# Moving the output gate of the last six expert rows to GpSimd, and the residual add to TensorE

## The chip, the cores and the metric

The program runs on one core of a Trainium2 chip. The metric is the device time of one execution in microseconds (us). TensorE is called PE, VectorE DVE, ScalarE ACT, GpSimd Pool, and the engine that only starts transfers here SP. PE's two clock levels are 1.2 and 2.4 GHz; a granted clock of 1.00 is the higher one.

## The reference, cut to what matters

Two transformer blocks over 256 tokens of width 1024. Only the very end of the second block is touched: a product-key mixture of single-neuron experts, its gated addition to the residual, and the last norm.

```python
def peer_ffn(h, ...):                      # 8 heads, 16 picks each, 16384 experts
    ...
    def chunk(args):                       # 128 tokens
        xc, ec, wc = args
        u = expert_u[ec]
        a = jax.nn.gelu(jnp.einsum('cd,chkd->chk', xc, u), approximate=False) * wc
        return jnp.einsum('chk,chkd->cd', a, expert_v[ec])
...
x = x + gt2[:, None, :] * peer_ffn(modulate(rmsnorm(x, norm2_g), sh2, sc2), ...)
return rmsnorm(x, final_g)
```

So each token needs 8 x 16 = 128 expert rows (u and v side by side, 2 x 1024 floats), a dot product of the u half with the token, a weight, and a weighted sum of the v halves; the sum is multiplied by the gate vector gt2, added to the residual, and the row is normed.

## The kernel before, in words

The first 870 us are two dense blocks and the attention of the second. Then comes the stage of the expert rows. The work is cut into 16 *units*: unit j is head j % 8 of token block j // 8 (128 tokens, one to a partition). A unit has 16 *picks*. For each pick Pool starts one indirect transfer (`fetch`, L2172) that brings for each of the 128 tokens its own row of 8 KB: 1 MB a pick, 256 picks in all. The rows land in 16 buffers (names in the rows: `arena`, `ring`, `rows_w`, `rows_x`, `rows_s`, `rows_l`); Pool may start a fetch when PE has read the pick that held the buffer before.

For each pick, in this order:

- DVE multiplies the u half with the token's vector and sums it (`dots`, L2014, a custom operation that reads two operands in SBUF).
- ACT takes the gelu of the sums of a group of picks (L1456), and DVE multiplies it with the softmax gate (`weigh`, L2025).
- ACT turns the weight of each token into a 128 x 128 diagonal matrix (`activate`, L1463; the diagonals lie in the buffers `silu` and `pT`).
- PE multiplies this diagonal with the v half in two halves of 512 columns (`weigh`, L1053 and L1057), and the sums grow in two PSUM banks: 4 and 5 for the first token block, 6 and 7 for the second. The fp32 product runs as two passes, so each half is two records.

Picks are taken in groups of 4, in the last unit in groups of 4, 2, 2, 2, 2, 1, 1, 1, 1 (`pick_groups`).

The order is written out by hand on each engine. PE's picks run in loops (`Fori`) of one unit a turn. Early in the stage `turn_residual` (L1046) transposes the residual h of both token blocks into banks 0 to 3. For the first token block, `total(0)` and `scaled_first` run between later units. For the second, after the last pick, `total(1)` on DVE takes for each half of 512 columns the sum from PSUM times the gate row (`gtrow`, in the tile `small`; L2036) and adds the turned residual from PSUM (L2037); ACT squares and sums the result (`finish`, L1472) and takes the root (L1477); DVE multiplies the row by the final gain (`fgrow`, L2059), inverts the root (L2047) and scales one half (L2063), ACT scales the other (L1528); SP and ACT each start one half's output transfer (L477, L1530).

Before this change Pool's last instruction is the start of the last fetch.

Of the kernel before, what the change touches and what calls it, by code (L numbers as in the profile page):

```python
# [14 lines left out]
P = 128  # L15
T = 256
TB = T // P
D = 1024
# [122 lines left out]
LOOPED = 2  # L141
assert all(HOMES[g][0] == HOMES[g - TK][0] for g in range((LOOPED + 1) * TK, UNITS * TK))

# [53 lines left out]
def program(nc, a, out):  # L197
    with ExitStack() as ctx:
# [181 lines left out]
        def _(sp):  # L380
# [96 lines left out]
            sp.dma_start(out[P:T, 0:512], out_rows[:, 1, 0:512]).then_inc(S("stored"), 16)  # L477
# [4 lines left out]
        def _(pe):  # L482
# [558 lines left out]
            def turn_residual():  # L1041

                pe.wait_ge(S("banks_freed"), S_END)
                for b in range(TB):
                    for c in range(C):
                        last = nc.tensor.transpose(ps[:, 2 * b + c // 4, (c % 4) * P:(c % 4 + 1) * P],  # L1046
                                                   h[:, c, b * P:(b + 1) * P], ident)
                last.then_inc(S("residual_turned"), 1)

            def weigh(acc, j, k, rows, first=False):  # L1050
# [4 lines left out]
                if k == TK - 1:  # L1055
# [33 lines left out]
            with pe.Fori(PH + 1, 2 * PH) as j:  # L1089
                weigh_unit(6, j)  # L1090


        @block.scalar
        def _(act):
# [370 lines left out]
            def finish(b):  # L1465
# [3 lines left out]
                for x in range(2):  # L1469
                    at = slice(x * 512, (x + 1) * 512)  # L1470
                    act.wait_ge(S("summed"), 2 * b + x + 1)
                    fn(squares[:, 2 * x:2 * x + 2, :], out_rows[:, b, at].rearrange("p (k n) -> p k n", k=2), ACT.Square,  # L1472
# [54 lines left out]
            act.wait_ge(S("gained"), 2)  # L1527
            fn(out_rows[:, 1, 512:D], e["junk"][:, 512:D], ACT.Copy, scale=lb[:, 7, 1:2]).then_inc(S("second_ready"), 1)  # L1528
            act.wait_ge(S("second_ready"), 1)
            act.dma_start(out[P:T, 512:D], out_rows[:, 1, 512:D]).then_inc(S("stored"), 16)  # L1530
# [3 lines left out]
        def _(dve):  # L1534
# [493 lines left out]
            def total(b):  # L2028

                for x in range(2):  # L2030
                    at = slice(x * 512, (x + 1) * 512)
                    if x == 0:
                        dve.wait_ge(S("half_weighed"), (b + 1) * PH)
                    else:
                        dve.wait_ge(S("weighed"), (b + 1) * PH * TK)
                    own(v.tensor_tensor(e["junk"][:, at], ps[:, 4 + 2 * b + x, :], gtrow[:, at], ALU.mult))  # L2036
                    own(v.tensor_tensor(out_rows[:, b, at], e["junk"][:, at], ps[:, 2 * b + x, :], ALU.add))  # L2037
                    dve.sem_inc(S("summed"), 1)

                dve.wait_ge(S("squares_summed"), 2 * b + 1)  # L2040
# [252 lines left out]
```

## Time and profile before

| | |
|---|---|
| median of three runs | 1518.01 us (1517.78 to 1518.86) |
| profiled execution, its own time | 1517.04 us |
| its span, first to last instruction | 1515.2 us |
| mean granted clock of PE | 0.975 |
| PE busy | 1372.2 us (91%) |
| DVE busy | 974.2 us (64%) |
| ACT busy | 554.8 us (37%) |
| Pool busy | 557.3 us (37%) |
| DMA, whole run | 427.03 MB, mean 282 GB/s |

The device time is 1.8 us longer than the span, which runs from the first to the last instruction seen. Busy shares are averages over stages with different limits; the change lies in the last 30 us, and what counts there is read from that stretch.

### The profile page before, as it was taken

To read this page: it belongs to the slowest core of one execution; us is meant where nothing else is said; L and a number is where in the kernel's file an instruction comes from. 1 tells how busy PE (TensorE), PEld (TensorE's weight loads), DVE (VectorE), ACT (ScalarE), POOL (GpSimd) and SP (SyncE) were. 2 spreads that over 40 slices of the span, in tenths; PEclk is the share of its full clock that TensorE was granted. 3 is DMA by queue.
4 is the path that set the end of the run, shared out by engine and by line. 5 is a ranking of instruction groups with operands and counts; after the bars stand their busy time and mean duration, and the time that the engine had idled before them with its cause. 6 is when DMAs were issued, how large, how long until landed. Compare 5 with 4: busy or idle time off the path is not lost.

```text
span 1515.2 us, 21160 instructions
## 1 busy us (share of the span) xinstructions
PE 1372.2 (91%) x7914; PEld 1048.4 (69%) x7914; DVE 974.2 (64%) x1877; ACT 554.8 (37%) x1008; POOL 557.3 (37%) x383
## 2 busy tenths in 40 slices
PE   9999999999999999999999999988777777787877
PEld 8999999979999999899999866433332333333332
DVE  3788464445688653465553676787777778777755
ACT  4444355425444444555563422221222223222212
POOL 3443546511344444200302344554444434443440
PEclk9999999999999999999999999999999999998999
DMA  6767764212577754235436599999999999999994
GB/s 235 261 248 260 278 240 145 105 56 91 202 262 250 250 191 143 85 126 181 142 116 271 202 421 421 420 421 422 422 422 422 421 421 422 422 422 421 421 422 189
DMA packets 59774, 427.03 MB, mean 282 GB/s; under 512 B 6640, under 2 KB 6960, under 8 KB 8624
## 3 DMA queue, kind: packets, MB, share of 16 engines
q0 software_dynamic: 36864, 268.45, 42.6%
q1 hardware_dynamic: 22176, 156.38, 28.8%
q10 hardware_dynamic: 656, 1.18, 0.2%
q8 instruction: 47, 0.77, 0.2%
q14 instruction: 31, 0.25, 0.1%
HBM read 424.93 MB, written 1.05 MB: 281 GB/s over the span
## 4 chain that ended last, share of the span: by engine, by line
PE 55%; DMA 24%; DVE 12%; issue 4%; ACT 3%; POOL 1%; DVEq 0%; ACTq 0%; POOLq 0%; SPq 0%
DMA rows_x<-in_expert_uv,arena 21%; PE ps L507 9%; PE ps L512 9%; PE ps L508 9%; PE ps L1053 5%; PE ps L1057 4%; DVE arena L2014 3%; PE ps L602 2%; PE ps L1009 2%; PE ps L604 2%; PE ps L603 2%; DVE arena L1648 2%; DMA arena<-in_expert_uv,arena 2%; DVE wlo L375 1%; PE ps L555 1%
## 5 line engine op out<-in xcount | busy, mean ns | idle before, releaser
L375 POOL TENSOR_TENSOR wlo<-ring,whi 128x1024 fp32r<-128x1024 f32 x102 | 253.7, 2490 | 445.3 <-ACT whi L1153 445.2
L1153 ACT ACTIVATE whi<-ring 128x1024 fp32r<-128x1024 f32 x220 | 228.6, 1056 | 317.3 <-PE ps L512 138.6
L507 PE MATMUL ps<-nh,whi 128*128 128x256 f32 x1312 | 330.4, 289 | 9.1 <-DVE wlo L375 3.4
L508 PE MATMUL ps<-nh,wlo 128*128 128x256 f32 x1312 | 323.1, 283 | 0.0
L375 DVE TENSOR_TENSOR wlo<-ring,whi 128x1024 fp32r<-128x1024 f32 x118 | 160.8, 1377 | 166.9 <-ACT whi L1153 162.4
L507 PEld LDWEIGHTS ps<-nh,whi 128*128 128x128 f32 x1312 | 251.2, 191 | 15.3 <-issue 5.2
L508 PEld LDWEIGHTS ps<-nh,wlo 128*128 128x128 f32 x1312 | 251.5, 192 | 0.1
L512 PE MATMUL ps<-nl,whi 128*128 128x256 f32 x1312 | 190.6, 285 | 0.0
L512 PEld LDWEIGHTS ps<-nl,whi 128*128 128x128 f32 x1312 | 171.3, 192 | 4.4 <-DVE nl L1586 0.6
L2014 DVE CUSTOM_DVE_ANT_0 arena<-arena 128x1024 f32<-128x1024 f32 x91 | 111.7, 1227 | 59.7 <-DMA arena<-in_expert_uv,arena 56.5
L2172 POOL DMA_INDIRECT arena<-in_expert_uv,arena x91 | 93.1, 1023 | 135.5 <-PE ps L1057 95.7
L1456 ACT ACTIVATE arena<-arena 128x4 f32<-128x4 f32 (+2 forms) x69 | 14.1, 205 | 313.1 <-DVEq L2016 313.1
L2172 POOL DMA_INDIRECT rows_w<-in_expert_uv,arena x68 | 72.6, 1068 | 116.8 <-PE ps L1057 82.6
L1648 DVE SCALAR_TENSOR_TENSOR arena<-arena,vec 128x256 f32<-128x256 f32 x168 | 106.4, 633 | 5.8
L2014 DVE CUSTOM_DVE_ANT_0 arena<-rows_w,arena 128x1024 f32<-128x1024 f32 x68 | 83.3, 1225 | 39.5 <-DMA rows_w<-in_expert_uv,arena 35.2
L602 PE MATMUL ps<-gh,whi 128*128 128x256 f32 x352 | 100.6, 286 | 0.3 <-DVE wlo L375 0.3
L604 PE MATMUL ps<-gl,whi 128*128 128x256 f32 x352 | 99.6, 283 | 0.0
L603 PE MATMUL ps<-gh,wlo 128*128 128x256 f32 x352 | 99.6, 283 | 0.0
L1053 PE MATMUL ps<-arena,silu 128*128 128x512 f32 x92 | 54.0, 671 | 37.0 <-ACT silu L1463 37.0
L602 PEld LDWEIGHTS ps<-gh,whi 128*128 128x128 f32 x352 | 67.5, 192 | 0.5 <-issue 0.5
L603 PEld LDWEIGHTS ps<-gh,wlo 128*128 128x128 f32 x352 | 67.5, 192 | 0.0
L604 PEld LDWEIGHTS ps<-gl,whi 128*128 128x128 f32 x352 | 67.5, 192 | 0.0
(347 smaller groups left out, 2364.9 us busy)
## 6 DMA issues: line engine op xcount, KB each, us to landing
ring<-in_w SPq DMA_DIRECT2D x112, 1024.0 KB, 4.9
arena<-in_wmod SPq DMA_DIRECT2D x24, 1024.0 KB, 4.9
arena<-in_w SPq DMA_DIRECT2D x6, 1024.0 KB, 9.0
small<-in_small SPq DMA_DIRECT2D x2, 938.5 KB, 6.9
arena<-in_expert_uv,arena POOLq DMA_INDIRECT x91, 25.6
rows_w<-in_expert_uv,arena POOLq DMA_INDIRECT x68
h<-in_x SPq DMA_DIRECT2D x2, 512.0 KB, 5.5
keys<-in_keys SPq DMA_DIRECT2D x1, 1024.0 KB, 8.0
```

Of the source, the lines that this page charges most:

```text
L375: return v.tensor_tensor(wlo[:, tile % TILES, :], ring[:, tile // 2 % RAW, at:at + TILE], whi[:, tile % TILES, :].bitcast(F32), ALU.subtract)
L507: mm(to, hi[:, k, :], nh[:, k, :], start=(k == 0), stop=False)
L508: mm(to, lo[:, k, :], nh[:, k, :], start=False, stop=False)
L512: last = mm(to, hi[:, k, :], nl[:, k, :], start=False, stop=(k == C - 1))
L602: mm(to, hi[:, w, :], gh[:, k, :], start=(k == 0), stop=False)
L603: mm(to, lo[:, w, :], gh[:, k, :], start=False, stop=False)
L604: last = mm(to, hi[:, w, :], gl[:, k, :], start=False, stop=(k == FC - 1))
L1053: half = mm(ps[:, acc, :], diagonal(k), rows[:, D:D + 512], start=first, stop=False, skip_group_check=True)
L1153: fn(whi[:, tile % TILES, :], ring[:, slot % RAW, at:at + TILE], ACT.Copy).then_inc(S("high_w"), 1)
L1648: own(v.scalar_tensor_tensor(to, wm[:, r, k, :], V("c", k), to, ALU.mult, ALU.add))
L2014: own(v.tensor_tensor_reduce(out=e["junk"], in0=expert_rows(g)[:, 0:D], in1=h2[:, j // PH, :], scale=1.0, scalar=0.0, op0=ALU.mult, op1=AL ...
L2172: nc.gpsimd.indirect_dma_start(buffer(home), None, a["expert_uv"], bass.IndirectOffsetOnAxis(ap=unit(j)["index"][:, k:k + 1], axis=0)).the ...
```

## The change

For the second token block alone:

- Pool, after its last fetch, multiplies the v half of each of the last six picks (`LATE` = 6, picks 10 to 15 of the last unit) in place by the gate row, in two pieces of 512 columns, each as soon as the row has landed.
- PE turns the residual of the second block with fp32 products against the identity, into banks 2 and 3, each opened by a product with zeros, so that these banks can be added to. The last unit is written out instead of being a turn of the loop. Its picks 0 to 9 go to banks 6 and 7 as before; the six late picks, already gated, go straight onto the residual in banks 2 and 3.
- DVE gates the sum of all other picks (`gated_last`, PSUM times `gtrow`) in two halves, after the weights of picks 10-11 and of pick 12, and PE adds them through the identity (`add_gated`) behind picks 12 and 13.
- After the last pick nothing has to be gated or added: ACT squares the row from PSUM, DVE multiplies the first half by the final gain beside it, and then scales the second half and gain in one operation; ACT scales the first half. The halves that SP and ACT store are swapped.

```diff
+LATE = 6
@@ tensor
-                for b in range(TB):
-                    for c in range(C):
-                        last = nc.tensor.transpose(ps[:, 2 * b + c // 4, (c % 4) * P:(c % 4 + 1) * P],
-                                                   h[:, c, b * P:(b + 1) * P], ident)
+                for c in range(C):
+                    nc.tensor.transpose(ps[:, c // 4, (c % 4) * P:(c % 4 + 1) * P], h[:, c, 0:P], ident)
+                for x in range(2):
+                    mm(ps[:, 2 + x, :], zeros[:, :], ones[:, :].unsqueeze(1).to_broadcast([P, 4, P]), start=True,
+                       stop=False, skip_group_check=True)
+                    for c in range(4):
+                        last = mm(ps[:, 2 + x, c * P:(c + 1) * P], h[:, 4 * x + c, P:T], ident, start=False, stop=False,
+                                  skip_group_check=True)
...
+            def weigh_late(k, rows):
+
+                for x in range(2):
+                    if x == 0:
+                        pe.wait_ge(S("diagonals"), (UNITS - 1) * TK + k + 1)
+                    pe.wait_ge(S("rows_scaled"), 2 * (k - TK + LATE) + x + 1)
+                    half = mm(ps[:, 2 + x, :], diagonal(k), rows[:, D + x * 512:D + (x + 1) * 512], start=False,
+                              stop=(k == TK - 1), skip_group_check=True)
+                    if x == 1:
+                        half.then_inc(S("weighed"), 1)
+                    elif k == TK - 1:
+                        half.then_inc(S("half_final"), 1)
+
+            def add_gated(x):
+
+                pe.wait_ge(S("summed"), 2 + x + 1)
+                mm(ps[:, 2 + x, :], ident, out_rows[:, 1, x * 512:(x + 1) * 512], start=False, stop=False,
+                   skip_group_check=True)
...
-            with pe.Fori(PH + 1, 2 * PH) as j:
+            with pe.Fori(PH + 1, 2 * PH - 1) as j:
                 weigh_unit(6, j)
+            for k in range(TK):
+                rows = expert_rows((UNITS - 1) * TK + k)
+                if k < TK - LATE:
+                    weigh(6, UNITS - 1, k, rows)
+                else:
+                    weigh_late(k, rows)
+                if k in (TK - 4, TK - 3):
+                    add_gated(k - TK + 4)
@@ scalar, finish(1)
+                    whole = ps[:, 2 + x, :] if b else out_rows[:, 0, at]
+                    fn(squares[:, 2 * x:2 * x + 2, :], whole.rearrange("p (k n) -> p k n", k=2), ACT.Square,
                        accum_out=lb[:, 4 + b, x:x + 1]
                        ).then_inc(S("squares_summed"), 1)
...
@@ vector
+            def gated_last(x):
+
+                at = slice(x * 512, (x + 1) * 512)
+                if x == 0:
+                    dve.wait_ge(S("half_weighed"), 2 * PH)
+                else:
+                    dve.wait_ge(S("weighed"), UNITS * TK - LATE)
+                v.tensor_tensor(out_rows[:, 1, at], ps[:, 6 + x, :], gtrow[:, at], ALU.mult).then_inc(S("summed"), 1)
...
             def scaled_last():
 
-                for x in range(2):
-                    at = slice(x * 512, (x + 1) * 512)
-                    own(v.tensor_tensor(e["junk"][:, at], out_rows[:, 1, at], fgrow[:, at], ALU.mult))
-                    dve.sem_inc(S("gained"), 1)
+                first_half(1)
+                v.tensor_tensor(e["junk"][:, 0:512], ps[:, 2, :], fgrow[:, 0:512], ALU.mult).then_inc(S("gained"), 1)
                 inverse(1)
                 dve.sem_inc(S("inverted"), 1)
-                v.tensor_scalar(out_rows[:, 1, 0:512], e["junk"][:, 0:512], lb[:, 7, 1:2], None, ALU.mult
-                                ).then_inc(S("out_ready"), 1)
+                v.scalar_tensor_tensor(out_rows[:, 1, 512:D], ps[:, 3, :], lb[:, 7, 1:2], fgrow[:, 512:D], ALU.mult, ALU.mult
+                                       ).then_inc(S("out_ready"), 1)
...
                     weigh(j, q, first, size)
+                    if j == UNITS - 1 and q in (4, 5):
+                        gated_last(q - 4)
...
-            total(1)
             scaled_last()
@@ gpsimd
+            pool.wait_ge(S("turned_copied"), 4)
+            for k in range(TK - LATE, TK):
+                pick = (UNITS - 1) * TK + k
+                landed, n = rows_landed(pick)
+                pool.wait_ge(S(landed), n)
+                for x in range(2):
+                    half = expert_rows(pick)[:, D + x * 512:D + (x + 1) * 512]
+                    g.tensor_tensor(half, half, gtrow[:, x * 512:(x + 1) * 512], ALU.mult).then_inc(S("rows_scaled"), 1)
```

The end of Pool's program, before. The DMA rows are the starts of the last fetches.

```order
L2172 DMA arena<-in_expert_uv,arena 128x2048 x4
L2172 DMA rows_w<-in_expert_uv,arena 128x2048 x4
L2172 DMA arena<-in_expert_uv,arena 128x2048
L2172 DMA rows_x<-in_expert_uv,arena 128x2048
L198 UNCONDITIONAL_BRANCH
```

The same place now:

```order
L2221 DMA arena<-in_expert_uv,arena 128x2048 x4
L2221 DMA rows_w<-in_expert_uv,arena 128x2048 x4
L2221 DMA arena<-in_expert_uv,arena 128x2048
L2221 DMA rows_x<-in_expert_uv,arena 128x2048
L2236 TENSOR_TENSOR rows_w<-rows_w,small 128x512 x8
L2236 TENSOR_TENSOR arena<-arena,small 128x512 x2
L2236 TENSOR_TENSOR rows_x<-rows_x,small 128x512 x2
L199 UNCONDITIONAL_BRANCH
```

Twelve operations with two operands in SBUF stand behind the last fetch, two for each late pick.

The end of DVE's program, before, from the dot product of the last pick on (`ISA` is the custom dot operation and the read of its sum; `lb` holds the norm's single columns, `h` the finished rows):

```order
L2014 ISA arena<-rows_x,arena 128x1024
L2014 ISA arena 128x1
L2025 SCALAR_TENSOR_TENSOR arena<-arena 128x1
L2036 TENSOR_TENSOR arena<-ps,small 128x512
L2037 TENSOR_TENSOR h<-arena,ps 128x512
L2036 TENSOR_TENSOR arena<-ps,small 128x512
L2037 TENSOR_TENSOR h<-arena,ps 128x512
L2041 TENSOR_SCALAR lb<-lb 128x1
L2059 TENSOR_TENSOR arena<-h,arena 128x512 x2
L2047 RECIPROCAL lb<-lb 128x1
L2063 TENSOR_SCALAR h<-arena,lb 128x512
```

The same place now, with the rows from pick 12 on:

```order
L2092 TENSOR_TENSOR h<-ps,small 128x512
L2052 ISA arena<-rows_w,arena 128x1024
L2052 ISA arena 128x1
L2063 SCALAR_TENSOR_TENSOR arena<-arena 128x1
L2092 TENSOR_TENSOR h<-ps,small 128x512
...
L2063 SCALAR_TENSOR_TENSOR arena<-arena 128x1
L2069 TENSOR_SCALAR lb<-lb 128x1
L2108 TENSOR_TENSOR arena<-ps,arena 128x512
L2097 RECIPROCAL lb<-lb 128x1
L2111 SCALAR_TENSOR_TENSOR h<-ps,lb,arena 128x512
```

Two of DVE's four operations on gate and residual moved ahead, around pick 12; the two adds went to PE; of the last scaling, two operations of 512 columns are left.

The end of PE's program now, where before each pick was a loop turn of L1053 and L1057:

```order
L1071 MATMUL ps<-rows_w,silu 128x512 x4
L1071 MATMUL ps<-rows_w,pT 128x512 x2
L1081 MATMUL ps<-h,con 128x512
L1071 MATMUL ps<-rows_w,pT 128x512 x2
L1081 MATMUL ps<-h,con 128x512
L1071 MATMUL ps<-arena,pT 128x512 x2
L1071 MATMUL ps<-rows_x,pT 128x512 x2
```

PE got two products more among the last picks (L1081), one behind pick 12 and one behind pick 13.

## Rows read from the trace of the kernel before

**Rows 1.** Windows view: stretch, length, five engines' busy us, granted clock, DMA share, GB/s

```profile
1100.00:1490.00 390.00, 306.91 (x628) 125.91 (x626) 274.04 (x642) 87.69 (x238) 160.54 (x150) 0.93 1.01 422
1498.00:1500.00 2.00, 2.00 (x6) 0.93 (x5) 1.45 (x3) 0.30 (x2) 0.00 (x0) 1.00 0.06 25
```

**Rows 2.** DMA queues from 870 to 1503 us: packets, MB, share

```profile
q14 instruction: 16, 0.13, 0.1%
q8 instruction: 4, 0.07, 0.0%
```

**Rows 3.** Timeline of DVE in the last unit, picks 10, 11, 14, 15

```profile
1490.70 1.23 DVE L2014 CUSTOM_DVE_ANT_0 arena<-rows_w,arena 128x1024 f32<-128x1024 f32 x1 [0.70 <-DMA rows_w<-in_expert_uv,arena]
1493.16 1.22 DVE L2014 CUSTOM_DVE_ANT_0 arena<-rows_w,arena 128x1024 f32<-128x1024 f32 x1 [1.23 <-DMA rows_w<-in_expert_uv,arena]
...
1500.56 1.23 DVE L2014 CUSTOM_DVE_ANT_0 arena<-arena 128x1024 f32<-128x1024 f32 x1 [0.69 <-DMA arena<-in_expert_uv,arena]
...
1503.03 1.23 DVE L2014 CUSTOM_DVE_ANT_0 arena<-rows_x,arena 128x1024 f32<-128x1024 f32 x1 [0.68 <-DMA rows_x<-in_expert_uv,arena]
...
1504.59 0.22 DVE L2025 SCALAR_TENSOR_TENSOR arena<-arena 128x1 f32<-128x1 f32 x1 [0.33 <-ACT arena L1456]
```

**Rows 4.** Timeline of PE, the two halves of the last pick

```profile
1505.29 1.12 PE L1053 MATMUL ps<-rows_x,pT 128*128 128x512 f32 x2 [0.47 <-ACT pT L1463]
...
1506.26 1.02 PE L1057 MATMUL ps<-rows_x,pT 128*128 128x512 f32 x2
```

**Rows 5.** Timeline of DVE and ACT behind the last pick

```profile
1506.45 0.69 DVE L2036 TENSOR_TENSOR arena<-ps,small 128x512 f32<-128x512 f32 x1 [1.65 <-PE ps L1053]
...
1508.74 0.69 DVE L2037 TENSOR_TENSOR h<-arena,ps 128x512 f32<-128x512 f32 x1
1509.52 0.63 ACT L1472 ACTIVATE small<-h 128x512 f32<-128x512 f32 x1 [0.84 <-DVEq L2038]
...
1510.27 0.29 ACT L1477 ACTIVATE lb<-lb 128x1 f32<-128x1 f32 x1
1511.31 0.16 DVE L2047 RECIPROCAL lb<-lb 128x1 f32<-128x1 f32 x1
1511.57 0.72 ACT L1528 ACTIVATE h<-arena,lb 128x512 f32<-128x512 f32 x1 [1.00 <-DVEq L2062]
...
1512.32 0.36 ACTq L1530 DMA_DIRECT2D out<-h  x1
```

**Rows 6.** Pool's two-operand operations: timeline, line (min/median/max ns), by form, line

```profile
735.54 3.50 POOL L2156 TENSOR_TENSOR small<-small,inv_count 128x256 f32<-128x256 f32 x4
...
L2156 POOL TENSOR_TENSOR small<-small,inv_count x4: 725/737/1071, 735.5 to 738.0; 128x256 f32<-128x256 f32 x4
...
L2150 POOL TENSOR_TENSOR small<-small 128x512 f32<-128x512 f32 x1 | 1.0, 1041 | 0.1
L375 POOL TENSOR_TENSOR wlo<-ring,whi x102: 2345/2410/3658, 17.5 to 817.0; 128x1024 fp32r<-128x1024 f32 x102
```

**Rows 7.** DVE and Pool at once: two timeline stretches, and two DVE lines over the run

```profile
80.09 4.56 DVE L375 TENSOR_TENSOR wlo<-ring,whi 128x1024 fp32r<-128x1024 f32 x2 [0.67 <-DVE arena L1648]
81.14 2.43 POOL L375 TENSOR_TENSOR wlo<-ring,whi 128x1024 fp32r<-128x1024 f32 x1 [2.00 <-ACT whi L1153]
...
104.56 3.85 DVE L375 TENSOR_TENSOR wlo<-ring,whi 128x1024 fp32r<-128x1024 f32 x2 [0.64 <-DVE arena L1648]
107.45 3.22 POOL L375 TENSOR_TENSOR wlo<-ring,whi 128x1024 fp32r<-128x1024 f32 x1 [1.26 <-ACT whi L1153]
...
L375 DVE TENSOR_TENSOR wlo<-ring,whi x118: 1206/1226/3428, 16.5 to 806.6; 128x1024 fp32r<-128x1024 f32 x118
L1631 DVE TENSOR_TENSOR silu<-silu,ps 128x512 f32<-128x512 f32 x22 | 14.9, 678 | 0.6 <-PE ps L512 0.6
```

**Rows 8.** The turning of the residual on PE, and fetches of 955 to 985 us to landing

```profile
961.78 1.91 PE L1046 MATMUL ps<-con,h 128*128 128x128 f32 x16
...
rows_x<-in_expert_uv,arena POOLq DMA_INDIRECT x2, 12.3
```

More of the change, by code:

```diff
@@ L476, in _ @@
             sp.wait_ge(S("out_ready"), 2)
-            sp.dma_start(out[P:T, 0:512], out_rows[:, 1, 0:512]).then_inc(S("stored"), 16)
+            sp.dma_start(out[P:T, 512:D], out_rows[:, 1, 512:D]).then_inc(S("stored"), 16)
             sp.wait_ge(S("stored"), 16 * 3)
@@ L1054, in weigh @@
                           skip_group_check=True)
-                if k == TK - 1:
+                if k == (TK - 1 if acc == 4 else TK - LATE - 1):
                     half.then_inc(S("half_weighed"), 1)
@@ L1470, in finish @@
                     at = slice(x * 512, (x + 1) * 512)
-                    act.wait_ge(S("summed"), 2 * b + x + 1)
-                    fn(squares[:, 2 * x:2 * x + 2, :], out_rows[:, b, at].rearrange("p (k n) -> p k n", k=2), ACT.Square,
+                    if b == 0:
+                        act.wait_ge(S("summed"), x + 1)
+                    elif x == 0:
+                        act.wait_ge(S("half_final"), 1)
+                    else:
+                        act.wait_ge(S("weighed"), UNITS * TK)
+                    whole = ps[:, 2 + x, :] if b else out_rows[:, 0, at]
+                    fn(squares[:, 2 * x:2 * x + 2, :], whole.rearrange("p (k n) -> p k n", k=2), ACT.Square,
                        accum_out=lb[:, 4 + b, x:x + 1]
@@ L1526, in _ @@
             act.wait_ge(S("inverted"), 1)
-            act.wait_ge(S("gained"), 2)
-            fn(out_rows[:, 1, 512:D], e["junk"][:, 512:D], ACT.Copy, scale=lb[:, 7, 1:2]).then_inc(S("second_ready"), 1)
+            act.wait_ge(S("gained"), 1)
+            fn(out_rows[:, 1, 0:512], e["junk"][:, 0:512], ACT.Copy, scale=lb[:, 7, 1:2]).then_inc(S("second_ready"), 1)
             act.wait_ge(S("second_ready"), 1)
-            act.dma_start(out[P:T, 512:D], out_rows[:, 1, 512:D]).then_inc(S("stored"), 16)
+            act.dma_start(out[P:T, 0:512], out_rows[:, 1, 0:512]).then_inc(S("stored"), 16)
         @block.vector
@@ L2026, in weigh, with first_half, total_first @@
                                        ).then_inc(S("weights"), 1)
-            def total(b):
+            def first_half(b):
+                dve.wait_ge(S("squares_summed"), 2 * b + 1)
+                v.tensor_scalar(lb[:, 6 + b, 2:3], lb[:, 4 + b, 0:1], 1.0 / D, EPS, ALU.mult, ALU.add
+                                ).then_inc(S("first_half"), 1)
+            def total_first():
                 for x in range(2):
@@ L2091, in _ @@
                     dve.wait_ge(S("final_landed"), 16)
-                    total(0)
+                    total_first()
                 if j == PH + 2:
                     scaled_first()
-            total(1)
             scaled_last()
```

13 lines of the change are left out of this document (6 added, 7 removed).

## The prediction

> **What bounds the kernel now.** I read the windows view first. From 1100 to 1490 us the DMA engines are busy all the time (share 1.01, 422 GB/s), while PE, DVE and Pool all have idle time [rows 1]. So the stage of the expert rows goes at the pace of the transfers: 256 rows of 1 MB. The starts of DVE's dots say the same at the end: picks 10 and 11 start 2.46 us apart, 14 and 15 start 2.47 apart, each behind a wait for DMA [rows 3].
>
> The end of that stage has a second limit. From 1498 to 1500 us the DMA share is 0.06 [rows 1], one engine of sixteen: fifteen are done and one still brings its part of the last rows. A row is 128 packets of 8 KB, 8 on each engine, so that engine takes 2.47 / 8 = 0.31 us a packet. The 20 instruction loads of the stage [rows 2] are not spread like the rows. If they all fall on one engine, 16 of 0.31 us and 4 of twice the size make 7.4 us, about the lag seen. So **the last row lands when this engine is through**, at 1503.0, and no work on PE or DVE moves that.
>
> Behind the last landing there is only a chain. The dot starts at 1503.03 and the weight at 1504.59 [rows 3]; PE starts the last pick at 1505.29, and its second half ends at 1506.26 + 1.02 = 1507.28 [rows 4]. DVE, ACT and DVE then gate, add, square, root, invert and scale, until the output transfer is started at 1512.32 [rows 5]. What the change can win is a part of these 5.0 us behind PE. **What it can lose is the time at which the last pick is finished.**
>
> **Part 1: the tail behind PE gets shorter.** Now ACT squares the second half from PSUM as soon as PE is done: 0.75 us from the start of a square to the start of the root, 0.29 for the root [rows 5]. Then about 0.1 for the hop to DVE, 0.16 for the inverse, 0.1 hop, 0.72 for ACT's scaling, 0.03 to the start of the transfer. The hops are those between 1511.31, 1511.57 and 1512.32 [rows 5]. DVE's gain product of 0.69 lies beside the square and the root. Sum with hops 2.2 us, against 1512.32 - 1507.28 = 5.04 before. Gain: **2.8 us**.
>
> **Part 2: Pool's twelve products.** Two questions: what does one cost, and can it run beside DVE?
>
> Price of a 128x512 product on Pool: a product of 256 columns took 725 ns undisturbed, a subtraction of 1024 columns 2.41 us in the median, an addition of 512 columns 1.04 us [rows 6]. No row shows a product of 512. Two times the product of 256 gives 1.45 us, the upper end; the addition is the lower end, 1.04. A line through 256 columns at 0.725 and 1024 at 2.41 gives 1.28 us at 512. I take **1.28**, since it lies between the product itself and the operation of the same kind that ran 102 times. Between two Pool operations lie (3.50 - 0.725 - 2 x 0.737 - 1.071) / 3 = 0.08 us [rows 6]. The Trainium skill, "GPSIMD Engine Reference", section 3.1, gives 4497 ns for a two-input add of 2048 fp32 columns. A quarter is 1.12 us, an estimate; by it the sum below would end at +2.3 us instead of +4.5.
>
> Beside DVE: in two places Pool and DVE both ran an operation with two operands in SBUF [rows 7]. At 80.09 two DVE operations of 1.23 took 4.56 us together; the second ended at 84.65, 1.08 behind Pool's end at 83.57. It did nothing while Pool worked, except for the last 0.14 us. At 107.45 it went the other way: Pool took 3.22 instead of 2.41, and DVE had ended at 108.41, so Pool stood still until then less 0.14 us at its start. DVE's product with one operand in PSUM stays at 678 ns on average [rows 7]. So such operations take turns, whole ones. DVE's dot of 1.23 us was never beside a Pool product before; it too reads the row and the token's vector from SBUF, and I count it as one that takes turns. The skill says the same more widely ("SBUF — State Buffer", section "Who interferes with whom"): a DVE instruction with two SBUF inputs contends with a GpSimd instruction that reads SBUF, and the later one is fully blocked. If that did not hold for the dot, rival B below would be the outcome.
>
> The walk. Pick 10 has landed when its dot starts at 1490.70 [rows 3], and the dot has the turn first. Pool is free long before. From here Pool always has a landed row to work on, because a row needs at least 2 x (1.28 + 0.08) = 2.72 us and rows land every 2.47. Each of the six dots holds Pool up once: by 1.23 - 0.14 = 1.09 us where the dot came just ahead (picks 10, 11, 14, 15), by 1.23 - 0.14 - 0.08 - 0.14 = 0.87 where it had waited for Pool's end (picks 12, 13). Together 6.14 us. The weights of 0.22 us fit into the gaps between Pool's operations. Pool's last product ends at
>
> 1490.70 + 12 x 1.28 + 11 x 0.08 + 6.14 = **1513.1 us**.
>
> DVE's dots are delayed too (the last weight comes at about 1507.7 instead of 1504.8), but that is no longer last. PE's last half then ends at 1513.1 + 0.04 + 1.12 = 1514.3, against 1507.28: **+7.0 us**. What waits for Pool is PE and nobody else; the fetches are all issued before.
>
> **Part 3: PE's additions at the end.** Two products through the identity, about 1 us each as the second half in [rows 4], behind picks 12 and 13. PE now waits for Pool's pieces, on average 22.3 / 12 = 1.9 us apart, and has 1.0 to do for each, so this costs nothing. If Pool did not bind, PE would: the idle 0.47 us before the last pick [rows 4] would be used up, and the last pick would start 0.6 us late. DVE's two gatings of 0.69 us read PSUM and so need no turn; they lie in the 0.68 us of waiting before a dot [rows 3] and are caught up before the last one.
>
> **Part 4: turning the residual.** 16 transposes took 1.91 us [rows 8]. Now eight transposes (0.96), eight two-pass products (1.91 at most) and two openings of 512 columns (1.02 each): 4.9 us, 3.0 more. It delays the freeing of a buffer and so one fetch by 3 us, but a fetch there lands 12.3 us after its start [rows 8] because five rows are queued ahead of it. Cost nothing; without that queue it would be up to 3 us.
>
> **Part 5: code.** PE's last unit is now straight code instead of a loop turn, and Pool has twelve operations more. One or two more instruction loads in this stage are likely, 0.31 us each on the late engine. I take **+0.3**, between 0 and 0.7.
>
> Sum: -2.8 + 7.0 + 0.3 = **+4.5 us**. From the profiled execution's 1517.04 us this is 1521.5. The median of the runs is 1.0 higher, 1518.01; on it the forecast is **1522.5 us**.
>
> **The rivals.** A difference below 0.2% (3.0 us) can hardly be told from none here, so "slower" begins at 1521.05 and "faster" ends at 1515.0.
>
> - A, the forecast: turns with the dot, a price near 1.28. With 1.20 the sum is +3.6, with 1.36 about +5.4. Chance 0.55.
> - B, not slower: the dot and Pool's products run beside each other. Then Pool's chain has only its own 12 x 1.36 = 16.3 us, ends at 1507.0, and PE's last half at about 1508.1; with the shorter tail that is -2.0 + 0.3 = -1.7 us, **1516.3 us**. For it: no row has a Pool product beside this custom operation. Against it: rows 7, for operations with the same operands. The point where it decides: Pool's row must not take more than some 2.5 to 3 us with everything that holds it up. With turns it takes 3.7. Chance 0.13.
> - C, turns, but the product costs what the addition does, 1.04 us: pieces start to wait for landings, and the walk gives +1.1 + 0.3, **1519.4 us**. The gain and loss of the change would cancel at about 0.93 us a product. For it: the row of the addition. Against it: 725 ns for 256 columns is already 70% of it. Chance 0.17.
> - D, dearer: 1.45 us a product gives 12 x 0.17 = 2.0 more, or PE at its lower clock in the tail: **1524.5 us**. Chance 0.15.
>
> **How the numbers follow.** The likeliest is A, 1522.5. The range reaches down over A to part of C and leaves out B, and reaches up over D: 1518.5 to 1525.5. Slower by over 0.2%: four fifths of A and nearly all of D and a little of C, 0.62. Within 0.2%: the rest of A, most of C and B, 0.34. Faster by over 0.2%: B with every term at its good end, 0.04.
>
> **What would show it.** In the profile after: Pool's products should take 1.28 us alone and about 2.3 where a dot came first; from pick 12 on, dots should take up to 1.7 us instead of 1.23. The wait before PE's last products should be for Pool, not for the diagonal. The first dots should start where they did, within 0.7 us. Pool's last product should end at about 1513, and the output transfer start 2.2 us behind PE's last half. The prediction is wrong if dots stay at 1.23 with Pool busy beside them (B), if a product takes 1.04 (C), or if anything before 1490 us has moved by more than 1 us.

## The result, and the profile after

| | before | with the change |
|---|---|---|
| median of 22 runs each | 1517.11 us (1513.74 to 1520.06) | 1520.24 us (1517.34 to 1525.63) |
| ratio of the runs | 1 | 1.0026, 95% interval 1.0019 to 1.0033 |
| profiled execution, its own time | 1517.04 us | 1519.11 us |
| span | 1515.2 us | 1517.3 us |
| start of pick 10's dot in the last unit | 1490.70 us | 1490.00 us |
| last output transfer started | 1512.32 us | 1514.20 us |

The kernel became slower by 3 to 4 us (the ratio says 1517.11 x 0.0026 = 3.9, the medians 3.1). The forecast was +4.5, and 1522.5 us for the median; 1520.24 lies inside its range of 1518.5 to 1525.5. The medians of before here (1517.11) and at the time of the forecast (1518.01, three runs) differ by themselves.

To keep the drift of whole runs out, I read each trace by one stretch: **from the start of pick 10's dot to the start of the last output transfer**. It was 1512.32 - 1490.70 = 21.62 us and is now 1514.20 - 1490.00 = 24.20 us: +2.6. (The expectations below say 24.12 for it, the start of ACT's transfer; SP's comes 0.08 later.) The 0.7 us by which pick 10 came sooner in this trace was there before the stage of the expert rows: its first dot started at 863.10 instead of 863.85, where both programs are alike.

DVE in the profile after, the rows that answer to [rows 3], from the timeline (L2052 is the dot, L2063 the weight, L2092 the new gating):

```profile
1490.00 1.23 DVE L2052 CUSTOM_DVE_ANT_0 arena<-rows_w,arena 128x1024 f32<-128x1024 f32 x1 [0.71 <-DMA rows_w<-in_expert_uv,arena]
...
1492.47 2.19 DVE L2052 CUSTOM_DVE_ANT_0 arena<-rows_w,arena 128x1024 f32<-128x1024 f32 x1 [1.24 <-DMA rows_w<-in_expert_uv,arena]
...
1495.72 0.68 DVE L2092 TENSOR_TENSOR h<-ps,small 128x512 f32<-128x512 f32 x1
1496.32 1.77 DVE L2052 CUSTOM_DVE_ANT_0 arena<-rows_w,arena 128x1024 f32<-128x1024 f32 x1
...
1499.75 1.77 DVE L2052 CUSTOM_DVE_ANT_0 arena<-rows_w,arena 128x1024 f32<-128x1024 f32 x1
...
1504.86 1.21 DVE L2052 CUSTOM_DVE_ANT_0 arena<-rows_x,arena 128x1024 f32<-128x1024 f32 x1
...
1506.40 0.80 DVE L2063 SCALAR_TENSOR_TENSOR arena<-arena 128x1 f32<-128x1 f32 x1 [0.33 <-ACT arena L1488]
```

Three dots take 2.19, 1.77 and 1.77 us instead of 1.23, and each of the five weights from pick 11 on takes 0.80 or 0.81 instead of 0.22 (the last of them is shown). The gating, which reads PSUM, takes its usual 0.68. The last dot starts 14.85 us behind pick 10's; before it was 12.33.

Pool's new products, by line with min/median/max in ns:

```profile
L2236 POOL TENSOR_TENSOR rows_w<-rows_w,small x8: 1260/2236/2311, 1490.1 to 1502.6; 128x512 f32<-128x512 f32 x8
L2236 POOL TENSOR_TENSOR arena<-arena,small x2: 1262/1786/2310, 1504.9 to 1507.1; 128x512 f32<-128x512 f32 x2
L2236 POOL TENSOR_TENSOR rows_x<-rows_x,small x2: 1255/1258/1260, 1508.4 to 1509.6; 128x512 f32<-128x512 f32 x2
```

Two prices and little between them: 1.26 us alone, 2.23 to 2.31 where a dot held the product up. The last two, behind DVE's last dot and weight, are undisturbed. (The eighth of the first eight ends at 1504.91; in the chain of waits below `POOLq L199` stands in its place.)

PE, ACT and DVE at the end, the rows that answer to [rows 4, 5]:

```profile
1507.33 2.26 PE L1071 MATMUL ps<-arena,pT 128*128 128x512 f32 x4 [0.38 <-POOL arena L2236]
1509.78 2.25 PE L1071 MATMUL ps<-rows_x,pT 128*128 128x512 f32 x4 [0.19 <-POOL rows_x L2236]
```

```profile
1512.07 0.60 ACT L1510 ACTIVATE small<-ps 128x512 f32<-128x512 f32 x1 [0.47 <-PE ps L1071]
...
1512.79 0.29 ACT L1515 ACTIVATE lb<-lb 128x1 f32<-128x1 f32 x1
1513.37 0.72 ACT L1566 ACTIVATE h<-arena,lb 128x512 f32<-128x512 f32 x1 [0.29 <-DVEq L2110]
1514.12 0.39 ACTq L1568 DMA_DIRECT2D out<-h  x1
```

PE's last picks wait for Pool, not for the diagonal, and end at 1509.78 + 2.25 = 1512.03. From there it is 2.1 us to ACT's transfer, where it had been 5.04. PE had also lost its higher clock on the way: the late dot of pick 11 let it stand for 2.80 us before 1496.28 (the wait for the diagonals of picks 10 and 11), and behind that the windows view grants it only 0.50, the lower level:

```profile
1498.00:1500.00 2.00, 2.00 (x3) 0.67 (x2) 1.67 (x5) 0.60 (x2) 2.00 (x2) 0.50 0.06 25
```

It costs nothing here. PE is through with pick 13 and the second addition at 1506.95 and then waits for Pool, and from 1505 us on the clock is 1.00 again.

The chain of waits of the last stretch (start, length, what) is short and names one engine:

```profile
1490.12 12.52 POOL rows_w L2236 x7
1502.64 2.27 POOLq L199
1504.91 3.50 POOL arena L2236 x2
1508.41 1.23 POOL rows_x L2236
1509.64 0.14 issue
1509.78 1.10 PE ps L1071 x2
```

From 1490.12 to 1509.64 the chain never leaves Pool. It does not show why Pool takes so long; the two prices above and the runs below do.

### The profile page after: what moved, and what is told of

The parts are those of the page before. It is cut to its first block, busy times and chain, and to the rows that moved or that the text cites. A ratio compares the mean times of both kernels' runs of the same rounds, so it can differ in the third digit from the quotient of the medians.

```text
span 1517.3 us, 21186 instructions
## 1 busy us (share of the span) xinstructions
PE 1375.7 (91%) x7930; PEld 1051.1 (69%) x7930; DVE 975.5 (64%) x1874; ACT 554.9 (37%) x1008; POOL 582.2 (38%) x395
## 3 DMA queue, kind: packets, MB, share of 16 engines
HBM read 424.93 MB, written 1.05 MB: 281 GB/s over the span
## 4 chain that ended last, share of the span: by engine, by line
PE 54%; DMA 26%; DVE 10%; issue 4%; ACT 3%; POOL 3%; POOLq 0%; DVEq 0%; ACTq 0%; SPq 0%
DMA rows_w<-in_expert_uv,arena 23%; PE ps L508 9%; PE ps L513 9%; PE ps L509 8%; PE ps L1058 5%; PE ps L1062 5%; DMA ring<-in_w 3%; PE ps L1010 2%; DVE arena L2052 2%; DVE arena L1686 1%; PE ps L603 1%; PE ps L605 1%; PE ps L604 1%; POOL wlo L376 1%; DVE wlo L376 1%
## 5 line engine op out<-in xcount | busy, mean ns | idle before, releaser
L376 DVE TENSOR_TENSOR wlo<-ring,whi 128x1024 fp32r<-128x1024 f32 x118 | 156.7, 1342 | 168.5 <-ACT whi L1185 163.3
L2052 DVE CUSTOM_DVE_ANT_0 arena<-arena 128x1024 f32<-128x1024 f32 x91 | 111.6, 1226 | 58.6 <-DMA arena<-in_expert_uv,arena 55.4
L1488 ACT ACTIVATE arena<-arena 128x4 f32<-128x4 f32 (+2 forms) x69 | 14.1, 205 | 314.3 <-DVEq L2054 314.3
L2052 DVE CUSTOM_DVE_ANT_0 arena<-rows_w,arena 128x1024 f32<-128x1024 f32 x68 | 85.4, 1255 | 38.2 <-DMA rows_w<-in_expert_uv,arena 33.8
```

The costliest lines, as they stand in the source:

```text
L376: return v.tensor_tensor(wlo[:, tile % TILES, :], ring[:, tile // 2 % RAW, at:at + TILE], whi[:, tile % TILES, :].bitcast(F32), ALU.subtract)
L2052: own(v.tensor_tensor_reduce(out=e["junk"], in0=expert_rows(g)[:, 0:D], in1=h2[:, j // PH, :], scale=1.0, scalar=0.0, op0=ALU.mult, op1=AL ...
```

## The experiments

Theory: a DVE operation and a Pool operation that both read two operands in SBUF take turns, whole operations, so six dots and twelve products stand in one line. Rival: Pool's products are just too slow for rows that land every 2.47 us, and the dots have no part in it. A second question was my reading of the late DMA engine.

**Dots that read PSUM.** `h2` of the second block is copied once to the free PSUM banks 0 and 1 (`vector_copy`):

```diff
                 if j == PH + 2:
                     scaled_first()
+                    own(v.tensor_copy(vector_copy, h2[:, 1, :]))
...
-    in1=h2[:, j // PH, :], scale=1.0,
+    in1=vector_copy if j == UNITS - 1 else h2[:, j // PH, :], scale=1.0,
```

> The changed kernel, but in the last unit the dot reads the token's vector from a copy in PSUM banks 0 and 1, so that it has one operand in SBUF. Measured by the stretch from the start of pick 10's dot to the start of the last output transfer: 21.62 us before, 24.12 with the change. Theory (dot and Pool product take turns because both read two operands in SBUF): the dots stay near 1.23 us beside Pool's products, Pool's twelve products end about 17 us after the dot of pick 10 instead of 20.85, and the stretch is about 20.1 us, 4 less than with the change and 1.5 less than before. Rival (Pool's twelve products are simply too slow, the dots do not matter): the products end as late as with the change and the stretch stays within 0.5 us of 24.1.

Measured: stretch **20.02 us**; 1513.88 us against 1515.26 for the kernel before on the same chip, ratio 0.9993 (0.9984 to 1.0002). Against the kernel before the gain of 1.6 us in the stretch is not clear of noise in the whole time; against the change it is (1.0019 to 1.0033 there). Pool's products end 14.89 us behind pick 10's dot, 2 us sooner than expected: twelve products of 1.26 to 1.28 us, none held up. DVE's dots and Pool's first pieces, from the timeline:

```profile
1491.39 1.22 DVE L2054 CUSTOM_DVE_ANT_0 arena<-rows_w,ps 128x1024 f32<-128x1024 f32 x1 [1.24 <-DMA rows_w<-in_expert_uv,arena]
...
1494.53 1.20 DVE L2054 CUSTOM_DVE_ANT_0 arena<-rows_w,ps 128x1024 f32<-128x1024 f32 x1
```

```profile
1489.05 9.86 POOL L2239 TENSOR_TENSOR rows_w<-rows_w,small 128x512 f32<-128x512 f32 x8 [16.84 <-DMA rows_w<-in_expert_uv,arena]
```

Eight products in 9.86 us, where the change needed 14.79 for the same eight. Nothing about Pool was edited; one operand of DVE moved. The rival has fallen. (The dot at 1494.53 is late because the weight before it, which still reads two operands in SBUF, took 1.05 us instead of 0.22.)

**No products on Pool.** The loop and PE's wait for it are taken out; the late picks' rows are added without the gate, which leaves that part of the computation out.

```diff
-                    pe.wait_ge(S("rows_scaled"), 2 * (k - TK + LATE) + x + 1)
...
-            for k in range(TK - LATE, TK):
+            for k in range(0):
```

> The changed kernel without Pool's products and without the wait for them: the six late picks are added ungated. All else of the change stays (tail, additions through the identity, straight last unit). Theory: everything that the change loses is lost to Pool's products, so the stretch from pick 10's dot to the last output transfer is 19.2 us, 2.4 less than before (21.62). Rival (the two additions on PE or DVE's two gatings between the dots cost something of their own): 20 us or more.

Measured: stretch **19.19 us** (one execution, 1513.55 us). The rest of the change wins 2.4 us net. What it loses, from 19.19 to 24.20, it loses to Pool's products: 5.0 us. The rest is not quite free, though: PE's last product ends 17.02 us behind pick 10's dot, and before it was 16.58.

```profile
1504.55 1.88 PE L1070 MATMUL ps<-rows_x,pT 128*128 128x512 f32 x4
```

PE enters this last pick without a pause, where before it had waited 0.47 us [rows 4]. With Pool out of the way PE is what ends last, and its two additions cost 0.4 us of the 2.9 us that the shorter tail wins.

**Products that nobody waits for**, in the kernel before:

```diff
+            for k in range(TK - 6, TK):
...
+                for x in range(2):
+                    half = expert_rows(pick)[:, D + x * 512:D + (x + 1) * 512]
+                    own(g.tensor_tensor(keys[:, 4 * x:4 * x + 4, :].rearrange("p a n -> p (a n)"), half,
+                                        gtrow[:, x * 512:(x + 1) * 512], ALU.mult))
```

> The kernel before, and behind the last fetch Pool multiplies the same twelve halves with the gate row into an unused buffer; nobody waits for it. Theory (taking turns): Pool's products end near 22.7 us after the start of pick 10's dot instead of 16.0 for twelve undisturbed ones, several dots take 1.3 to 2.2 us instead of 1.23, and the last weight is 0.5 to 1.5 us late, and the transfer with it. Rival (no turns, the products are only slow): the products end at 16.0, all dots take 1.23 us, and the stretch of 21.62 us does not move.

Measured (one execution, 1517.0 us): Pool's products end at 21.72 us, where 22.7 was expected with turns and 16.0 without; one dot takes 2.31 us, and the weights 0.80. The last weight ends 15.0 us behind pick 10's dot instead of 14.1. The stretch is 24.26, 2.6 us longer, more than the late weight explains. Two more things are in it. DVE's gain products in the tail, two operands in SBUF again, took turns too: 2.08 us for the two, 1.52 before. And PE fell behind, because its clock was low behind a pause of 2.92 us (the wait for the diagonals of picks 10 and 11, before 1494.42):

```profile
1509.05 2.08 DVE L2059 TENSOR_TENSOR arena<-h,arena 128x512 f32<-128x512 f32 x2
```

```profile
1496.00:1498.00 2.00, 2.00 (x4) 0.88 (x3) 1.67 (x4) 0.61 (x2) 1.92 (x2) 0.50 0.06 25
1498.00:1500.00 2.00, 2.00 (x5) 0.85 (x4) 1.67 (x4) 0.60 (x2) 1.92 (x2) 0.77 0.06 25
```

(Windows view, columns as in [rows 1].) The granted clock is 0.50 from 1496 to 1498 us, the lower of the two levels, and PE works on to the end without a pause. So the products alone delay DVE, though nobody needs them; by how much this stretch would have grown at the higher clock stays open.

**Three late picks.** LATE = 3, DVE's gatings behind the weights of picks 13 and 14, PE's additions behind picks 13 and 14.

```diff
-LATE = 6
+LATE = 3
...
-                if k in (TK - 4, TK - 3):
-                    add_gated(k - TK + 4)
+                if k in (13, 14):
+                    add_gated(k - 13)
...
-                    if j == UNITS - 1 and q in (4, 5):
-                        gated_last(q - 4)
+                    if j == UNITS - 1 and q in (6, 7):
+                        gated_last(q - 6)
```

> The changed kernel with LATE = 3: Pool gates picks 13 to 15 only; DVE's two gatings stand behind the weights of picks 13 and 14, PE's additions behind picks 13 and 14. Theory: with half the products Pool is through sooner, its last product ends near 18 us after the start of pick 10's dot (20.85 with the change), and the stretch to the last output transfer is 21.3 us, 2.8 less than with the change and 0.3 less than before. Rival (the gatings of DVE, now nearer to the last dot, and the additions make up for it): 22.5 us or more.

Measured: stretch **21.27 us**, Pool's last product at 17.83; ratio 1.0004 (0.9995 to 1.0013). Half the products take most of the loss away; against the kernel before (21.62 us) the whole time shows no difference. The products still alternate between 1.26 and 2.24 us:

```profile
L2236 POOL TENSOR_TENSOR arena<-arena,small x2: 1262/1752/2242, 1499.1 to 1501.3; 128x512 f32<-128x512 f32 x2
```

**Four late picks and dots from PSUM, first try.** LATE = 4 and the PSUM copy; the gatings stayed behind the weights of picks 10-11 and of pick 12.

> The changed kernel with both findings: LATE = 4 (gatings and additions where the change has them, around picks 12 and 13) and the dots of the last unit reading the token's vector from PSUM. Theory: Pool's eight products run beside the dots and are through before PE needs them, so the stretch from pick 10's dot to the last output transfer is 19.6 us (21.62 before, 24.12 with the change, 20.0 with six late picks and the PSUM copy), and the time is 2 us below the kernel before. Rival (with four late picks the gating of DVE waits for pick 11 on PE and pushes the last dots back): 20.3 us or more.

Measured: stretch **24.30 us**, ratio 1.0008 (0.9999 to 1.0017). The theory missed and its rival came true: with four late picks the sum to be gated includes picks 10 and 11, whose diagonals come only after the weight that DVE has just sent. DVE's timeline shows it standing:

```profile
1492.77 0.22 DVE L2065 SCALAR_TENSOR_TENSOR arena<-arena 128x2 f32<-128x2 f32 x1 [0.33 <-ACT arena L1488]
1496.75 0.69 DVE L2094 TENSOR_TENSOR h<-ps,small 128x512 f32<-128x512 f32 x1 [3.76 <-PE ps L1058]
```

3.76 us of waiting for PE, with pick 12's dot queued behind. PE in turn stands for 2.88 us until pick 12's diagonal comes, and then works at the lower clock level (timeline of PE, and windows view with columns as in [rows 1]):

```profile
1500.46 3.56 PE L1071 MATMUL ps<-rows_w,pT 128*128 128x512 f32 x4 [2.88 <-ACT pT L1495]
```

```profile
1500.00:1502.00 2.00, 1.54 (x2) 0.83 (x3) 1.71 (x3) 0.60 (x2) 2.00 (x2) 0.56 0.01 4
1502.00:1504.00 2.00, 2.00 (x4) 0.82 (x3) 1.64 (x4) 0.60 (x2) 1.64 (x2) 0.58 0.00 0
```

The four records of a late pick take 3.56 us here and 1.88 at the higher clock. A wait that is free with one number of late picks costs all of the gain with another, here by itself and by the clock that PE loses in the pause.

**The same with the gatings in the right place**, behind the weights of picks 12 and 13 (`q in (5, 6)`; PE as with the change):

> The run with four late picks and dots from PSUM again, but DVE's two gatings stand where PE has their picks done: behind the weights of picks 12 and 13 (there they stood behind the weights of picks 10-11 and of pick 12, and DVE waited for pick 11 on PE). Theory: the stretch from pick 10's dot to the last output transfer is 19.6 us (21.62 before, 20.0 with six late picks and the PSUM copy), the time 2 us below the kernel before. Rival (one of the two gatings still comes too late): 20.3 us or more.

Measured: stretch **19.55 us**, 1513.32 us against 1515.24 on the same chip, ratio 0.9989 (0.9979 to 0.9998). PE's first late pick starts 8.26 us behind pick 10's dot, where it was 11.70 in the run before, and the clock stays at 1.00. Of the 4.75 us between the two runs, 3.4 are the later start and 1.7 the low clock, less some 0.4 of short pauses of PE that only the faster run has.

**The late DMA engine.** Before, one engine of sixteen brought the last rows alone [rows 1]. I compare the time at which the last 8 KB packet of the stage starts, counted from the start of the first dot, from the packets in the trace: 638.39 us before and 638.44 with the change. Four edits to the kernel before change only the amount of straight code.

> The kernel before with two semaphore increments more behind each dot on DVE, that nobody waits for: 512 instructions more in the stage, some 4 loads of 8 KB more. Theory (loads of DVE's code delay the late DMA engine by about 1 us each): the last packet of the stage comes 4 us later, 642.4 us after the first dot instead of 638.4. Rival (0.31 us a load): 639.6. Rival (no connection): 638.4.

> The kernel before with two semaphore increments more behind each diagonal on ACT, that nobody waits for: the same 512 instructions more as in the run before, on another engine, some 4 loads of 8 KB more. If the loads of all engines go over the late DMA engine: last packet 1.2 to 4 us later than 638.4 after the first dot. If ACT's loads go over another one, which the lag suggests by not growing at 1194 and 1322 us: 638.4, within 0.5.

> The kernel before, only that each dot signals the counter that ACT waits for itself, and DVE waits on that counter, instead of signalling its own counter and raising the other in an instruction of its own: 256 DVE instructions fewer in the stage of the expert rows, nothing else. Theory (the last row is late because one DMA engine also carries instruction loads, those of DVE's straight code among them, about 1 us each by the growth of the lag at 1052, 1108, 1163, 1221, 1277 us): two loads of 8 KB fewer, so the last 8 KB packet of the stage comes about 636.4 us after the first dot instead of 638.4, and the time is 1 to 2 us shorter. Rival (a load costs no more than its own 0.31 us): 637.8. Rival (the lag has nothing to do with loads): 638.4.

> The kernel before, only that each dot writes its products over the u half that it reads (nobody reads it again) and signals ACT's counter itself, so that no dot has to wait for the one before it: one DVE instruction fewer per pick, 256 in the stage, which the run with self-counting dots did not reach (its trace has 28 fewer). Theory (each 8 KB load of DVE's code costs the late DMA engine 0.9 us, as 512 more instructions did with 4 loads and 3.7 us): 2 loads fewer, the last packet 636.5 us after the first dot instead of 638.4, and the time 1.9 us shorter. Rival (the lag is only added to by more code, what is there now has another cause): 638.4 and no gain.

The edits, in this order:

```diff
                     dve.sem_inc(S("dotted"), 1)
+                    dve.sem_inc(S("idle_count"), 1)
+                    dve.sem_inc(S("idle_count"), 1)
```

```diff
                     fn(diagonal(g), ident, ACT.Copy, scale=u["w"][:, k:k + 1]).then_inc(S("diagonals"), 1)
+                    act.sem_inc(S("idle_count"), 1)
+                    act.sem_inc(S("idle_count"), 1)
```

```diff
-                    own(v.tensor_tensor_reduce(... accum_out=u["dots"][:, k:k + 1]))
-                    dve.sem_inc(S("dotted"), 1)
+                    v.tensor_tensor_reduce(... accum_out=u["dots"][:, k:k + 1]).then_inc(S("dotted"), 1)
+                    dve.wait_ge(S("dotted"), g + 1)
```

```diff
-                    own(v.tensor_tensor_reduce(out=e["junk"], ... accum_out=u["dots"][:, k:k + 1]))
-                    dve.sem_inc(S("dotted"), 1)
+                    v.tensor_tensor_reduce(out=expert_rows(g)[:, 0:D], ... accum_out=u["dots"][:, k:k + 1]).then_inc(S("dotted"), 1)
```

| edit | DVE / ACT instructions in the trace | 8 KB loads in the stage | last packet behind first dot | against before |
|---|---|---|---|---|
| none (kernel before) | 2550 / 1381 | 16 | 638.39 us | |
| more vector code | 3062 / 1381 | 20 | 642.07 us | +3.7 |
| more scalar code | 2550 / 1893 | 20 | 638.01 us | -0.4 |
| dots count themselves | 2522 / 1381 | 16 | 638.74 us | +0.4 |
| fewer vector instructions | 2294 / 1381 | 14 | 637.12 us | -1.3 |

The same can be read from the timelines of DVE, at the first and the last dot of the run with more vector code, and of the run with more scalar code:

```profile
861.60 1.23 DVE L2014 CUSTOM_DVE_ANT_0 arena<-rows_w,arena 128x1024 f32<-128x1024 f32 x1
...
1504.46 1.23 DVE L2014 CUSTOM_DVE_ANT_0 arena<-rows_x,arena 128x1024 f32<-128x1024 f32 x1 [0.67 <-DMA rows_x<-in_expert_uv,arena]
```

```profile
862.68 1.23 DVE L2016 CUSTOM_DVE_ANT_0 arena<-rows_w,arena 128x1024 f32<-128x1024 f32 x1
...
1501.48 1.23 DVE L2016 CUSTOM_DVE_ANT_0 arena<-rows_x,arena 128x1024 f32<-128x1024 f32 x1 [0.68 <-DMA rows_x<-in_expert_uv,arena]
```

642.86 us between the two dots with 512 more instructions on DVE, 638.80 with 512 more on ACT, 639.18 before [rows 3] (its first dot started at 863.85). Both have four more loads. So **the late engine carries the loads of DVE's code and not those of ACT's**.

What a load costs it is less plain than 3.7 us for four. With more vector code all DMA engines, not the late one alone, ran short of work for a while. The windows view shows it (columns as in [rows 1]), first before, then with 512 more instructions on DVE:

```profile
922.00:942.00 20.00, 19.88 (x65) 11.28 (x64) 17.40 (x43) 5.08 (x17) 10.60 (x9) 1.00 1.01 422
942.00:962.00 20.00, 18.53 (x60) 10.22 (x59) 12.08 (x31) 6.33 (x13) 8.33 (x8) 1.00 1.02 420
```

```profile
922.00:942.00 20.00, 18.78 (x60) 10.29 (x59) 16.02 (x40) 4.45 (x15) 10.34 (x9) 1.00 1.00 406
942.00:962.00 20.00, 18.53 (x61) 10.22 (x60) 12.31 (x28) 6.33 (x13) 7.49 (x8) 1.00 1.00 407
```

16 and 13 GB/s less over 20 us each are 1.4 us of transfers at 421 GB/s. The packets agree: half of the sixteen engines are still at work until 628.75 us behind the first dot before, and until 630.15 in this run, 1.4 later. That part is no load on the late engine; what held the fetches back there stays open. What is left for four loads is 2.3 us, **0.6 a load**, and the two loads removed give 0.6 to 0.7 each (half of the engines are at work until 628.85 there). It is twice the 0.31 us of a packet of a row. The theories of 1 and 0.9 us a load were too high, and the run with fewer instructions lies between its theory (636.5) and its rival (638.4). Each of these figures rests on one trace.

Loads do not explain the whole lag either. 512 instructions are four loads, so the 1401 of DVE between the first and the last dot are about 11, and 11 x 0.6 is 6.6 us, an estimate. The late engine's last packet starts 9.6 us behind the point at which half of the engines are through. The other 3 us are open.

The self-counting dots were no test: the wait took the place of the increment, and only 28 instructions went. The run with fewer instructions took 1513.8 us against 1515.24, ratio 0.9992 (0.9983 to 1.0). The self-counting dots took 1516.11 against 1514.86, ratio 1.0009 (1.0 to 1.0018); more vector and more scalar code took 1518.50 and 1515.51 us in one execution each. Differences of 0.4 us between last packets are near what two executions differ by: in six other traces here, with DVE's code in the stage nearly unchanged, the last packet came at 637.8 to 638.3 us.

**All together:** the change with four late picks in the right place, the last unit's dots from PSUM, and one DVE instruction fewer per pick.

> The change with four late picks in the right place, dots of the last unit from PSUM, and one DVE instruction fewer per pick (the two runs beside it together). Theory: the two gains lie in different stretches and add: 1.9 us before the last landing and 2.0 behind it, ratio about 0.9974 against the kernel before. Rival (they overlap): the gain of the better one alone, 2 us, 0.9987.

Measured: **1511.86 us** (1509.48 to 1515.23) against 1515.24, ratio **0.9976 (0.9967 to 0.9985)**; last packet at 636.04, stretch 19.60. Both gains are in it, and it beats the kernel before and the change. The last packet comes 2.35 us sooner than before, with the same two loads fewer that gave 1.3 by themselves; the 1.1 us between them are not explained. Its end on the timeline (SP's transfer, and the row of pick 10's dot):

```profile
1487.09 1.22 DVE L2054 CUSTOM_DVE_ANT_0 rows_w<-rows_w,ps 128x1024 f32<-128x1024 f32 x1 [0.77 <-DMA rows_w<-in_expert_uv,arena]
...
1506.69 0.34 SPq L478 DMA_DIRECT2D out<-h  x1
```

| run | stretch expected | measured | ratio to before |
|---|---|---|---|
| kernel before | | 21.62 | 1 |
| the change | (forecast 26.1) | 24.20 | 1.0026 |
| dots from PSUM | 20.1 | 20.02 | 0.9993 |
| no Pool products | 19.2 | 19.19 | one execution |
| products that nobody waits for | 22.1 to 23.1 | 24.26 | one execution |
| three late picks | 21.3 | 21.27 | 1.0004 |
| four late, PSUM, gatings too early | 19.6 | 24.30 | 1.0008 |
| four late, PSUM, gatings in place | 19.6 | 19.55 | 0.9989 |
| all together | 19.6 in it | 19.60 | 0.9976 |

## Why the prediction was right, point by point

- **What bounds the stage, and the tail: right in its main part.** The dots of the stage keep their pace with the change: from the first dot to pick 10's are 626.85 us before and 626.90 after. That the last landing hangs on one DMA engine is shown by the runs with more and with fewer DVE instructions. That all 20 instruction loads go over it was wrong: ACT's do not. The sum of 7.4 us was "about the lag seen" by luck: it took every load at its own packet time, where DVE's alone went over this engine, at about 0.6 us each, and the lag was 9.6.
- **Part 1, the shorter tail: right.** 5.04 - 2.1 = 2.9 us measured, 2.8 forecast.
- **Part 2, price of a product: right.** 1.26 us measured, 1.28 forecast. The estimate from the Trainium skill ("GPSIMD Engine Reference", section 3.1), 1.12 us, was too low for this product. (The terms of the walk give +2.6 us with 1.12 and +1.6 with 1.04, where the prediction has +2.3 and +1.4.)
- **Part 2, taking turns: right**, and it is what decided. The rule of the Trainium skill ("SBUF — State Buffer", section "Who interferes with whom"), that a DVE instruction with two SBUF inputs contends with a GpSimd instruction that reads SBUF, holds for the custom dot too, as the PSUM run shows by taking one operand away. The six hold-ups sum to 6.0 us (1.0 each); the forecast was 6.14, and its own terms sum to 6.10. They were spread differently, at 0.97 to 1.05 instead of 1.09 and 0.87.
- **Part 2, the weights: wrong, without effect on the sum.** They were to "fit into the gaps between Pool's operations". There are no gaps, and five weights took 0.80 us each. They delayed DVE and not Pool, and Pool was last. The last weight ended 17.2 us behind pick 10's dot, forecast 17.0.
- **Part 2, the term that was mis-sized: the gaps between products.** I had put 0.08 us between two Pool operations, 11 times. The records follow each other with an overlap of about 0.04 us: 12 x 1.26 + 6.0 is 21.1, and Pool's products took 20.7 in all. The row that I took the gap from was of operations that each wait for the one before; the products that nobody waits for, written the same way, have 0.08 us between them again. This term is 1.3 us too large, and with the price and the hold-ups 1.5 us in all: Pool's last product ended 20.85 us behind pick 10's dot, not 22.4.
- **Part 3, PE's additions and DVE's gatings: right** for six late picks: hidden behind Pool, and without Pool's products PE's end came 0.4 us later, forecast 0.6. The first try with four late picks shows what the gatings cost when placed one step too early.
- **Part 4, turning the residual: right.** On PE it took from 961.09 to 965.46 us, 4.4 us where I had 4.9, and the stage did not move.
- **Part 5, code: wrong.** One load of 16 KB more came, as expected, but the last packet moved by 0.05 us and not by 0.3. That load is PE's: it is there without Pool's products and not there with the products in the kernel before. In the five runs with it and PE's straight code unchanged the last packet came at 637.8 to 638.3 us, so PE's straight code does not load over the late engine.
- **The sum.** By the stretch +2.6 instead of +4.5: 1.5 from Pool's end, 0.3 from the code, 0.1 from the tail. By the ratio of the runs +3.9, by the medians +3.1. The half to one and a half us between the trace and the many runs is open; PE's low clock reaching into the tail in some executions, as it did with the products that nobody waits for, is a possible cause that was not tested. So the time came nearer to the forecast than the mechanism earned, and that part is luck.
- **The rivals.** B (no turns) fell with dots of 2.19 us and products of 2.31. C (1.04 us a product) fell with 1.26, though its time of 1519.4 lies nearer to the measured 1520.24 than 1522.5 does. Of D, the low clock did come, at 0.50 from 1498 to 1500 us, but too early to cost anything in the execution that was profiled.

## What to carry to other kernels

Before work is moved to Pool "because it is idle", count the operands in SBUF on both sides: a two-operand product there cost 1.26 us for itself and 1.0 us more where it met a dot of DVE that read two, and it held DVE's dots and weights up in turn (the weights, 0.22 us long, cost Pool nothing: with the dots in PSUM its products took 1.26 to 1.29). Moving one operand of DVE to PSUM gave 4.2 us back where removing half of Pool's work gave 2.9. And a wait on another engine has to be placed anew each time the number behind it changes: here 4.75 us, over a third of it because PE paused and came back at the lower clock.

## What the runs showed of the hardware that was not expected

- Straight code on DVE costs transfer time at the end of a long DMA-bound stage: 512 instructions more, none of them busy work, delayed the last of 256 rows of 1 MB by 3.7 us, about 2.3 of it on the one late engine; the same number on ACT delayed nothing (one execution each).
- Removing one instruction per pick from DVE brought the last packet 1.3 us sooner in one trace and 2.35 in the other, although DVE was busy only 70% of the time (274.04 of 390 us) [rows 1].
- A DVE weight of 128x1, 0.22 us of work, took 0.80 us with Pool's products beside it, and up to 1.07 in the run with four late picks. Short operations pay the whole remaining time of the long one.
